# A fp32 decoder trunk on one core: the first down rows waited for by another semaphore, one weight unit split later, wider bias bands, one norm row on another queue

## What is computed

```python
for layer in range(DEPTH):                      # DEPTH = 2
    g = norm_gains[layer]
    h = rms_norm(x, g[0])
    if layer < N_A_LAYERS:                      # layer 0
        h = mixer_a(h, w_qkv_a[layer], w_o_a[layer])
    else:                                       # layer 1
        if layer == N_A_LAYERS:
            shared_kv = shared_kv_from(x, g_kv, w_kv_b)
        h = mixer_b(h, shared_kv, w_q_b[j], w_o_b[j], rel_bias)
    x = x + rms_norm(h, g[1])
    h = swiglu(rms_norm(x, g[2]), w_gate_up[layer], w_down[layer])
    x = x + rms_norm(h, g[3])
# mixer_b: scores of each head get bias = rel_bias[relative_bucket(distance)], 3 groups of dilation
```

## Time and profile before

| | |
|---|---|
| median of 3 runs | 756.27 us (755.78 to 756.65) |
| profiled execution | 755.12 us |
| its span | 753.4 us |
| TensorE busy | 742.7 us, 99% |
| VectorE busy | 532.5 us, 71% |
| ScalarE busy | 415.7 us, 55% |
| GpSimd busy | 174.2 us, 23% |

### The profile page before, as it was taken

How to read it: one execution, slowest core, us unless ns; L and a number is a source line. 1 busy time by engine, 2 the same in 40 slices (tenths; PEclk the granted TensorE clock), 3 DMA queues, 4 the chain that set the end, 5 groups by cost and what they waited for, 6 DMA issues and landing times.

```text
span 753.4 us, 13349 instructions
## 1 busy us (share of the span) xinstructions
PE 742.7 (99%) x4608; PEld 638.8 (85%) x4608; DVE 532.5 (71%) x772; ACT 415.7 (55%) x619; POOL 174.2 (23%) x298
## 2 busy tenths in 40 slices
PE   9999999999999999999999999999999999999996
PEld 7999987878888888898898898898888788888884
DVE  5788997867666566778778778678657676556653
ACT  4866667444433433875866766858666453343331
POOL 1000001225100000137665665566402000000000
PEclk9999999999999999999999999999999999999998
DMA  8735585599857656569797886897843896675622
GB/s 247 209 117 165 180 242 192 175 283 266 241 188 218 213 182 176 147 166 240 197 225 182 203 211 160 193 224 219 242 140 98 261 276 191 229 232 190 209 56 57
DMA packets 192868, 147.69 MB, mean 196 GB/s; under 512 B 40632, under 2 KB 181536, under 8 KB 192832
## 3 DMA queue, kind: packets, MB, share of 16 engines
q1 hardware_dynamic: 153344, 131.45, 56.4%
q10 hardware_dynamic: 32704, 8.36, 6.4%
q0 software_dynamic: 6784, 7.41, 5.7%
HBM read 138.02 MB, written 1.11 MB: 185 GB/s over the span
## 4 chain that ended last, share of the span: by engine, by line
PE 89%; DVE 4%; DMA 3%; ACT 2%; issue 1%; ACTq 0%; SPq 0%; POOL 0%; DVEq 0%; POOLq 0%
PE ps L1281 18%; PE ps L1283 18%; PE ps L1282 18%; PE ps L1517 10%; PE ps L1519 5%; PE ps L1287 3%; PE ps L1289 3%; PE ps L1288 3%; DVE w_lo L857 2%; DMA raw<-in_w_down 1%; ACT w_hi L545 1%; PE ps L1358 1%; DMA work<-work 1%; PE ps L1375 1%; PE ps L1360 1%
## 5 line engine op out<-in xcount | busy, mean ns | idle before, releaser
L857 DVE TENSOR_TENSOR w_lo<-raw,w_hi 128x2048 fp32r<-128x2048 f32 (+2 forms) x144 | 279.4, 1957 | 82.9 <-ACT w_hi L545 82.9
L545 ACT ACTIVATE w_hi<-raw 128x2048 fp32r<-128x2048 f32 (+2 forms) x144 | 233.0, 1638 | 104.6 <-DVE work L1117 40.2
L1281 PE MATMUL ps<-w_hi,xt 128*128 128x512 f32 x352 | 137.9, 392 | 0.7 <-DVE work L1111 0.7
L1283 PE MATMUL ps<-w_hi,xt 128*128 128x512 f32 x352 | 137.1, 389 | 0.0
L1282 PE MATMUL ps<-w_lo,xt 128*128 128x512 f32 x352 | 137.0, 389 | 0.0
L452 POOL TENSOR_SCALAR stat<-stat 128x1 f32<-128x1 f32 x15 | 9.9, 659 | 407.9 <-ACT work L561 383.8
L719 ACT ACTIVATE work<-ps,stat 128x256 f32<-128x256 f32 x44 | 21.0, 476 | 135.1 <-PE ps L1283 132.9
L1281 PE MATMUL ps<-w_hi,ot 128*128 128x512 f32 x240 | 94.6, 394 | 0.0
L1282 PE MATMUL ps<-w_lo,ot 128*128 128x512 f32 x240 | 93.5, 390 | 0.0
L1283 PE MATMUL ps<-w_hi,ot 128*128 128x512 f32 x240 | 93.5, 389 | 0.0
L483 POOL DMA_DIRECT2D work<-bias_rows x128 | 73.4, 575 | 43.8 <-DVE ot L1134 27.2
(11 more groups left out here) (153 smaller groups left out, 1257.3 us busy)
## 6 DMA issues: line engine op xcount, KB each, us to landing
raw<-in_w_gate_up SPq DMA_DIRECT2D x88, 512.0 KB, 4.9
raw<-in_w_kv_b SPq DMA_DIRECT2D x96, 256.0 KB, 4.1
raw<-in_w_down SPq DMA_DIRECT2D x22, 1024.0 KB, 4.8
raw<-in_w_q_b SPq DMA_DIRECT2D x48, 256.0 KB, 4.3
raw<-in_w_qkv_a SPq DMA_DIRECT2D x23, 512.0 KB, 5.0
raw<-in_w_o_a SPq DMA_DIRECT2D x4, 1024.0 KB, 6.6
work<-bias_rows POOLq DMA_DIRECT2D x128, 32.0 KB, 3.4
raw<-in_w_o_b SPq DMA_DIRECT2D x4, 1024.0 KB, 5.2
```

The costliest lines, as they stand in the source:

```text
L545: act.activation(w_hi[:, s % CUT, 0:size(s)], raw[:, s % RAW, 0:size(s)], ACT.Copy).then_inc(hi_made, 1)
L857: dve.tensor_tensor(w_lo[:, c, 0:n], raw[:, s % RAW, 0:n], w_hi[:, c, 0:n].bitcast(F32), ALU.subtract).then_inc(lo_made, 1)
L1281: mm(out, xs[0], ws[0], start=start, stop=False)
L1283: return mm(out, xs[1], ws[0], start=False, stop=stop)
```

## The change

Four edits stand in one diff.

1. SP waits for the parted planes of a SwiGLU's first step, not for the turned ones, before it loads the first down rows.
2. At the entry to the second layer, unit `B0 + 3` is copied by ScalarE after the first two squares and split by VectorE after the last update, where both came before the squares and the first product.
3. A band of bias is loaded once for both token tiles, 96 words of 4 bytes wide in place of twice 64, always into the same buffers. Per head there are 8 issues in place of 12, and the loop over heads does not wait for `rows_done` any more.
4. The norm's row of the second layer's attention (`norm_gains[1, 1:2]`) is issued by ScalarE and has a semaphore of its own; GpSimd issued it.

```diff
+SPAN = RUN + HR * (NT - 1)          # 96
-                         [[(2 * R - 1) * 2 * RUN, NH], [1, HR], [HR, NT], [2 * RUN, R], [1, RUN]]) for r in range(R)]
+                         [[(2 * R - 1) * 2 * RUN, NH], [1, HR], [2 * RUN, R], [1, SPAN]]) for r in range(R)]
...
@@ SP: swiglu
-                sp.wait_ge(planes_turned, planes_at(l, 0))
+                sp.wait_ge(planes_made, 2 * l * STEPS + 2)
                 two_rows(s0 + 6, 0, down_dram[l][:, 0:2, :])
@@ GpSimd: head_bias
                 for r in range(R):
                     at_ = slice(HR * r, HR * r + HR)
-                    for t in range(NT):
-                        pool.dma_start(band[at_, t].rearrange("p (c n) -> p c n", c=R),
-                                       bands[r][ds(h, 1)][:, :, t].rearrange("h m c n -> (h m) c n")).then_inc(band_in, 16)
-                    pool.dma_start(own_[at_], own_bands[ds(h, 1)].rearrange("h m t n -> (h m) t n")
-                                   ).then_inc(band_in, 16)
-                pool.wait_ge(band_in, (h * 16 + 16) * (R * (NT + 1)))
+                    pool.dma_start(band[at_], bands[r][ds(h, 1)].rearrange("h m c n -> (h m) c n")).then_inc(band_in, 16)
+                    pool.dma_start(own_band[at_], own_bands[ds(h, 1)].rearrange("h m n -> (h m) n")).then_inc(band_in, 16)
+                pool.wait_ge(band_in, (h * 16 + 16) * (2 * R))
...
-            pool.wait_ge(rows_done, 2)
             with pool.Fori(0, PAIRS - 1) as j:
                 head_bias(0, j * 2 + 2)
                 head_bias(1, j * 2 + 3)
-            pool.wait_ge(pvb_done, PAIRS)
-            load_post(norm_gains[1, 1:2, :])
@@ ScalarE
             hi(B0 + 1)
             hi(B0 + 2)
+            square_h(1, 0, B0 - 1)
             hi(B0 + 3)
-
-            square_h(1, 0, B0 - 1)
             square_h(1, 1, B0 - 1, [0])
...
             hi(FB0 + 1)
+            act.wait_ge(pvb_done, PAIRS)
+            act.dma_start(post, norm_gains[1, 1:2, :].broadcast_to([P, D])).then_inc(post_act, 16)
             boundary(2, WOB0 + 3, 6)
@@ VectorE
-                dve.wait_ge(post_in, 16 * (b + 1))
+                dve.wait_ge(*((post_act, 16) if b == 2 else (post_in, 16 * (b + 1 if b < 2 else b))))
...
-            for u in range(1, 4):
-                lo(B0 + u)
+            lo(B0 + 1)
+            lo(B0 + 2)
             scale_h(1, 0)
...
             update(1, 1)
+            lo(B0 + 3)
             cut_xkv(1)
```

More of the change, by code:

```diff
@@ L53 @@
 CUT = 6
-WORK = 6912
+WORK = 6880
 HR = P // R
+SPAN = RUN + HR * (NT - 1)
 OWN = [(NG - 1) * HR * (t + 1) for t in range(NT)]
@@ L130, in build @@
         bands = [bass.AP(bias_rows.tensor, bias_rows.offset + 2 * RUN * r,
-                         [[(2 * R - 1) * 2 * RUN, NH], [1, HR], [HR, NT], [2 * RUN, R], [1, RUN]]) for r in range(R)]
+                         [[(2 * R - 1) * 2 * RUN, NH], [1, HR], [2 * RUN, R], [1, SPAN]]) for r in range(R)]
         own_bands = bass.AP(bias_rows.tensor, bias_rows.offset + 2 * RUN * (R - 1),
-                            [[(2 * R - 1) * 2 * RUN, NH], [1, HR], [HR, NT], [1, RUN]])
+                            [[(2 * R - 1) * 2 * RUN, NH], [1, HR], [1, SPAN]])
         raw = sb("raw", [P, RAW, UNIT])
@@ L210, in build @@
         bias = [carve(WS) for _ in range(2)]
-        band = carve(NT * SEQ).rearrange("p (t s) -> p t s", t=NT)
-        early_band, own_band = (v.rearrange("p (t n) -> p t n", t=NT) for v in (halves_in[:, 0:NT * RUN], ones[:, :]))
+        band = carve(R * SPAN).rearrange("p (c s) -> p c s", c=R)
+        own_band = carve(SPAN)
         low = ob[:, :, :].rearrange("p t n -> p (t n)")
@@ L247, in build @@
         zeros_made = sem("zeros_made")
+        post_act = sem("post_act")
         last_mean = sem("last_mean")
@@ L476, in head_bias @@
                 static = isinstance(h, int)
-                own_ = early_band if static else own_band
                 if not static or h >= 1:
@@ L498, in head_bias @@
                     to, blocked = part(bias[b], t), part(mask_b, t)
-                    distances = band[:, t, ::-1].rearrange("p (c u n) -> p u c n", c=R, u=NT)
+                    reach = slice(HR * t, HR * t + RUN)
+                    distances = band[:, ::-1, reach][:, :, ::-1].rearrange("p c (u n) -> p u c n", u=NT)
                     pool.tensor_tensor(to[0], blocked[0], distances[:, 0:t + 1], ALU.add)
-                    distances = own_[:, t:t + 1, ::-1].rearrange("p o (u n) -> p u o n", u=NT)
+                    distances = own_band[:, reach][:, ::-1].rearrange("p (o u n) -> p u o n", o=1, u=NT)
                     inst = pool.tensor_tensor(to[1], blocked[1], distances[:, 0:t + 1].broadcast_to(
```

## The result

| | before | after |
|---|---|---|
| median | 756.18 us (755.75 to 756.65, 8 runs) | 760.12 us (759.04 to 765.28, 8 runs) |
| ratio, 95% interval | | 1.0062 (1.0048 to 1.0075) |
| profiled execution | 755.12 us | 764.26 us |
| its span | 753.4 us | 762.6 us |

The change makes the kernel 3.9 us slower, 0.6%, clear of the noise; 755.0 was forecast, in a range from 754.0 to 756.3. The profiled execution is one of the longer ones, 4.1 us above its own median, so I read mechanisms from it, and what the change costs from the median.

A forecast was written before the change was run, and what follows sets the result against it. TensorE was taken to set the span of 753.4 us, with 2.21 us lost in three gaps. Gains of 0.53 + 0.47 + 0.27 + 0 + 0 = 1.27 us took the median 756.27 to 755.0, range 754.0 to 756.3.

The forecast's parts named there:

- the cost is 3.1 us of landing time, all of it covered: First SwiGLU step: transposition lands in 7.1 us beside down rows, 4.00 alone; up to 8.0 costs nothing.
- the following gate rows start earlier too: SwiGLU loads: no SP load behind the down rows would suffer, and the gate rows gain an earlier start.
- over 1 us as a sign of being wrong: SwiGLUs: prediction wrong if turned planes come later than VectorE asks for them by more than 1 us.
- Rival 4: SwiGLUs: transposition starves beside the megabyte, slower once landing takes over 8.0 us; 759.0 us at 10 us; chance 0.08.
- 0.60 forecast: First SwiGLU: ScalarE's copy of the down rows starts 0.60 us earlier, no longer waiting for the load.
- 0.94 forecast: Second layer's entry: of the closed 1.21 us gap, 0.94 returns as TensorE's wait for VectorE's cuts; gain 0.27.
- Rival 2: Second layer's entry: the late split hides, the boundary gives all of 1.21 us, time 754.05 us; chance 0.20.
- Gain 0: Second layer's attention norm row issued by ScalarE: gains 0, since TensorE has no wait there.
- The offset of 1.15: Whole kernel: profiled execution stands 1.15 us below the median 756.27; the same 1.27 us gain was taken from both.

The follow-up runs named there:

- e1_norm_late: Kernel before with first down rows loaded at the parted planes, and GpSimd's SwiGLU norm row held until the planes are turned: 754.72 us against 756.28.
- after_norm_late: Changed kernel with GpSimd's norm row of both SwiGLUs held until the planes are turned: 753.46 us against 756.47 for the kernel before.
- e1_gate_held: Kernel before with first down rows loaded at the parted planes, and SP's gate rows held until the planes are turned: 755.22 us against 756.28.
- after_norm_by_gpsimd: Changed kernel with the norm's row of the second layer's attention issued by GpSimd again: 762.06 us against 756.47 for the kernel before.
- e1_and_e4: Kernel before with first down rows loaded at the parted planes and the second layer's attention norm row issued by ScalarE: 757.34 us against 756.47.
- e1_only: Kernel before with only the first down rows loaded at the parted planes: 758.81 us against 756.28.
- e1_both_held: Kernel before with first down rows loaded at the parted planes, norm's row and gate rows both held until the planes are turned: 754.44 us against 756.13.
- e234: Changed kernel with the earlier load of the first down rows taken back, the other three edits kept: 755.85 us against 756.28 for the kernel before.
- e2_only: Kernel before with only the later copy and split of unit B0+3: 755.72 us against 756.36.
- gate_first: Kernel before with VectorE's second gate product of a SwiGLU's first step ahead of its split of the down rows, no load moved: 754.13 us against 756.13.
- no_wait: Kernel before without SP's wait for turned planes, so the first down rows load 0.86 us ahead of the transposition: 754.51 us against 756.13.

## Why the prediction was wrong

**The step that failed** is in the paragraph on what edit 1 adds: "With down rows in flight beside it a transposition of this size took 7.1 us to land", and from it "the cost is 3.1 us of landing time, all of it covered". The 7.1 is the transposition of the next step, beside which the down load is 0.69 us ahead (154.30 against 154.99) and GpSimd's row is over. In the first step there are the norm's row, issued at 137.70, and a load that starts with the transposition, not before it. Both issue times stand in the trace of before, and the sum does not use them. It also took the earlier gate rows for no harm ("the following gate rows start earlier too"); they are the other neighbour. Measured: 10.6 and 12.3 us, so the planes were 3.66 us late in the first SwiGLU where the prediction gave over 1 us as a sign of being wrong. The only row of that kind was taken for an upper bound, and it was the row of a milder case. Three things bring the landing back under 8.0 us, each by itself: a lead of 0.86 us for the load (6.6 to 7.1 in six transpositions of three kernels), the norm's row held (6.4 to 6.6 in four, of e1_norm_late and after_norm_late), the gate rows held (7.3 and 7.7 in e1_gate_held).

**Rival 4 had the threshold and the price, and half of the cause.** "It decides once it takes over 8.0 us to land": at 8.0 us TensorE lost nothing, at the four landings of 9.1 to 9.9 us in after_norm_by_gpsimd and e1_and_e4 0.95 to 1.79, at 10.1 us 2.02, at 10.6 us 2.51, at 12.3 us 4.14. But "beside the megabyte" is not enough, as e1_both_held shows; it takes the norm's row and the gate rows too. The time that it gives for 10 us in both layers is 759.0; the median is 760.1, and that is near by some luck, since the clock was not in it. It had 0.08, for the one reason that the slowest row spoke against it.

**The clock was in none of the cases.** After a gap of 2.5 and of 4.1 us (excess over the usual 0.23) TensorE was granted 1.2 GHz for 3.41 us, which cost 1.58 and 1.53 us; after the 3.7 us gap of after_norm_by_gpsimd it was the same. After the 2.02 us gap of e1_only it kept 2.4 GHz. So each of the three longer gaps cost some 1.5 us more than itself, and the shorter ones did not. Whether length or place decides it, the runs don't say. The two groups of e1_only's executions, with their two levels of mean clock, say that this is a part of its spread. By the mean clock five of e1_only's ten executions have such a stretch, and all eight of the changed kernel. The kernel before has a mean of 0.995 in five of its executions, which took 758.2 to 759.2 us, so it is not free of them either.

**Edit 1's own purpose was met.** ScalarE's copy of the down rows no longer waits for their load (0.57 us earlier, 0.60 forecast). The gain was there to be had: e1_norm_late takes it, at 1.6 us.

**Edit 2 was right.** The gap of 1.21 us at 306 is gone, and 0.93 comes back at the cuts (0.94 forecast): net 0.29 against 0.27. The mean took 0.30 us with no split beside it (0.29 taken), so of 0.29 and 0.70 us the right one was chosen. Rival 2 lost on its own ground, but its 1.21 were one place further in the order.

**Edits 3 and 4 at nothing were right, if at all, only as a pair.** GpSimd's waits for bands fell from 58.1 to 29.6 us, its busy time from 174.2 to 147.0, ScalarE's norm row came 3.7 us after its issue at 558.93, and TensorE has no wait for any of them. e234 and e2_only (755.85 and 755.72, 0.4 and 0.6 under their own kernels before) leave a few tenths either way. But "Gain 0" was wrong for edit 4 beside edit 3: the profiled execution of after_norm_by_gpsimd lost 5.2 us at the late row, after nothing. By the medians it is less, 5.6 us above the kernel before in place of 3.9, with intervals that overlap (3.6 to 7.5 and 3.6 to 5.7). Edit 3 was costed by its band waits alone, and not by what GpSimd does behind the loop.

**The offset of 1.15** between the profiled execution and the median was carried over as a constant. Part of it is probably not one: the landing of the first transposition and of the load behind it vary (gaps of 1.00 to 1.60 us together in three profiles), and the profile of before had the smallest sum. What gate_first won there in the median is 2.0 and not 1.0.

**What stays open.** Why the packets stall. In the first SwiGLU they do so with the norm's row in flight, before included (20 of 1056 over 150 ns), almost not with it held back (3 and 1), and less with the load 0.86 us ahead (29). What holds a packet up for a microsecond is not in the traces, and neither is what holds back the transposition's first packet. Why GpSimd's first issue behind the loop is late with edit 3 is open too; the profile names no releaser. And the changed kernel's median stays 1.3 us above e1_only's. Where it comes from is visible, a later second landing and clock lost in all executions in place of half, but it is not shown by a run that differs in this alone; the executions of e1_and_e4, e1_only and the changed kernel (medians 757.3, 758.8, 760.1) spread over 5 to 8 us each and overlap.

## What to carry to other kernels

A load moved up to start with a transfer that is on the critical path must be priced as contention with everything in flight at that moment, from the issue times on all queues; a row from a neighbouring step is not an upper bound, and where there is only one, the threshold's rival deserves a real share of the chance. Before moving a load to close a gap, ask what the late engine did first: here the split of rows that nobody needed yet stood ahead of the product that TensorE waited for, and changing the two places gave as much as the best form of the earlier load. And when one execution is profiled, gaps that hang on a transfer's landing are draws: compare them over several profiles before taking their sum as what can be won.

## What was not expected of the hardware

- A transposition of 256 KB within on-chip memory lands in 3.7 to 4.4 us beside the end of a norm's row, 6.2 to 6.4 beside 1 MB of loads, and 8.0 to 12.3 beside 1 MB, the gate rows and the norm's row. Its packets start 3.3 to 5.0 us after the issue when a load of 1 MB is issued with it, and 1.4 to 1.6 without (2.7 with the norm's row issued 0.45 us before).
- Issuing that same load 0.86 us before the transposition, not with it, brings this back to 6.6 to 7.1 us in six transpositions out of six.
- While it is slow, the 16 transfer engines show full occupation at 144 GB/s, where no_wait shows 316 in the same stretch: occupation does not tell that data moves.
- TensorE's granted clock went to 0.5 for 3.41 us behind gaps of 2.5, 3.7 and 4.1 us, in the middle of the kernel, at 1.5 to 1.6 us each, and not behind one of 2.02 us.
- GpSimd's first transfer after its loop was issued 2.6 to 3.4 us after its release in kernels with the wide bands, and at once in those with the narrow ones.
